# One decoder step: first unit of each feed-forward stage as eight plain products, and the second gated group brought in by quadrants

## The reference

```python
def conv_ffn(h, prev, w_up, conv_w, conv_b, w_down):
    l = h.shape[1]
    u = h @ w_up
    ext = jnp.concatenate([prev, u], axis=1)
    y = conv_b + sum(conv_w[k] * ext[:, k:k + l] for k in range(CONV_WIDTH))
    a, v = jnp.split(y, 2, axis=-1)
    return (jax.nn.silu(a) * v) @ w_down, ext[:, -(CONV_WIDTH - 1):]
```

## Time and profile before

| | |
|---|---|
| median of 3 runs | 3003.3 us (2996.12 to 3003.37) |
| the profiled execution | 3006.05 us |
| its span in the trace | 3004.0 us |
| its mean granted PE clock | 0.96 |
| PE busy | 2792.8 us, 93% |
| DVE busy | 1877.8 us, 63% |
| ACT busy | 1227.7 us, 41% |
| POOL busy | 1192.5 us, 40% |

### The profile page before, as it was taken

One profiled execution on the slowest core, in us unless ns is written; L12 is line 12 of the kernel. 1 busy time (PEld: TensorE's weight loads), 2 busy tenths in 40 slices (PEclk: granted clock), 3 DMA queues, 4 the chain that ended last, 5 costly groups with the idle time before them and its releaser, 6 DMA issues. The chain is left out here.

```text
span 3004.0 us, 54687 instructions
## 1 busy us (share of the span) xinstructions
PE 2792.8 (93%) x20984; PEld 2564.1 (85%) x20984; DVE 1877.8 (63%) x3428; ACT 1227.7 (41%) x2492; POOL 1192.5 (40%) x786
## 2 busy tenths in 40 slices
PE   8998979999989996999999799899978999998898
PEld 7996966666767796999999799897878999998898
DVE  6212148888545526788887766695356777777665
ACT  5002027777723314554545333314234455444332
POOL 4430000000000143445455778560334555547876
PEclk9999989999979998999999999999988999998999
DMA  6216750000357420222222222312101222232222
GB/s 187 55 42 229 238 179 4 2 2 2 126 153 220 131 78 24 71 81 83 69 83 105 100 87 70 133 41 116 43 31 58 83 71 85 83 108 103 82 79 88
DMA packets 163911, 272.16 MB, mean 91 GB/s; under 512 B 19510, under 2 KB 112028, under 8 KB 162480
## 3 DMA queue, kind: packets, MB, share of 16 engines
q1 hardware_dynamic: 137348, 225.19, 22.5%
q10 hardware_dynamic: 26316, 43.66, 4.4%
HBM read 226.22 MB, written 46.69 MB: 91 GB/s over the span
## 5 line engine op out<-in xcount | busy, mean ns | idle before, releaser
L3065 PE MATMUL banks<-token_blocks_high,weight_blocks_high 128*128 128x272 f32 x3696 | 780.5, 293 | 108.2 <-DVE x L3359 35.0
L3065 PE MATMUL banks<-token_blocks_low,weight_blocks_high 128*128 128x272 f32 x3696 | 771.4, 291 | 0.0
L3065 PE MATMUL banks<-token_blocks_high,weight_blocks_low 128*128 128x272 f32 x3696 | 771.3, 291 | 0.0
L3065 PEld LDWEIGHTS banks<-token_blocks_high,weight_blocks_high 128*128 128x128 f32 x3696 | 587.5, 192 | 120.0 <-issue 83.8
L3065 PEld LDWEIGHTS banks<-token_blocks_low,weight_blocks_high 128*128 128x128 f32 x3696 | 589.8, 192 | 0.0
L3065 PEld LDWEIGHTS banks<-token_blocks_high,weight_blocks_low 128*128 128x128 f32 x3696 | 587.4, 192 | 0.0
L2975 POOL TENSOR_TENSOR weight_blocks_low<-weights_again_whole,weight_blocks_high 128x512 fp32r<-128x512 f32 (+2 forms) x151 | 228.0, 1513 | 195.3 <-ACT weight_blocks_high L3089 195.0
L2975 POOL TENSOR_TENSOR weight_blocks_low<-weights_whole,weight_blocks_high 128x512 fp32r<-128x512 f32 (+2 forms) x151 | 217.6, 1447 | 204.2 <-ACT weight_blocks_high L3089 202.7
L3321 DVE SCALAR_TENSOR_TENSOR conv_space<-conv_space,conv_w 128x1024 f32<-128x1024 f32 x176 | 230.3, 1308 | 77.5 <-ACT conv_space L3146 66.0
L2975 POOL TENSOR_TENSOR weight_blocks_low<-ight_quarters_more,weight_blocks_high 128x512 fp32r<-128x512 f32 (+2 forms) x150 | 211.9, 1415 | 155.5 <-ACT weight_blocks_high L3089 154.6
L3359 DVE TENSOR_TENSOR x<-x,banks 128x544 f32<-128x544 f32 x224 | 160.4, 718 | 172.4 <-PE banks L3065 169.1
(11 more groups left out here) (512 smaller groups left out, 5310.8 us busy)
## 6 DMA issues: line engine op xcount, KB each, us to landing
gated_scratch<-conv_space ACTq DMA_DIRECT2D x44, 544.0 KB, 3.9
past_rows<-in_kv_pages SPq DMA_DIRECT2D x160, 128.0 KB, 2.4
ight_quarters_more<-in_w_up SPq DMA_DIRECT2D x56, 256.0 KB, 3.0
weights_whole<-in_w_up SPq DMA_DIRECT2D x56, 256.0 KB, 2.9
weights_again_whole<-in_w_up SPq DMA_DIRECT2D x56, 256.0 KB, 2.9
staged<-gated_scratch SPq DMA_DIRECT2D x8, 1632.0 KB, 8.6
z<-in_kv_pages SPq DMA_DIRECT2D x96, 128.0 KB, 2.4
x<-in_cmp_pages ACTq DMA_DIRECT2D x64, 128.0 KB, 5.8
```

Source lines behind the costliest of these rows:

```text
L3065: last = pe.matmul(out[:, piece, :], a[:, at], b[:, kk, piece * HP:(piece + 1) * HP], start=first and kk == 0 and z == 0, stop=kk == n - 1 ...
```

## The change

- **Unit 0** is made of 8 plain products: `first_unit` multiplies x1, x3, x2, x4 in this order with two quarters of weights each, 192 matmuls where 168 were. Its four weight blocks are plain quarters; `project` rounds and splits all four ahead of layer 0's stage and two ahead of layer 1's (`blocks_ready`), the other two come at the stage's start. Results go to `ext` by four copies of ACT (`copy_first`); there is no `place` for unit 0.
- The norm's multiplications and the tokens' low parts for unit 0 are made by rows and half quadrants (`norm_rows`, `lower_rows`). The four **token sums** are made behind them, for unit 1 on.
- **Unit 1** is no longer interleaved with unit 0; only units 20 and 21 are (`LEAD`, `LAST`). ACT does unit 0's two taps between the rounding of the third and fourth token sums, its silu and store during unit 1.
- **Weight sums** of unit 1 and of unit 21 are made by POOL (`SUMMED_BY_POOL`), those of units 2 to 20 by DVE as before.
- **Staging** of groups 1 to 3: four transfers, one per quadrant, each with its semaphore; DVE's and ACT's waits are for their own quadrant. The tables for the way from group 0 to group 1 have other numbers.
- Places in memory and bank numbers move (`UP_PLACE`, `DOWN_SLOTS`, `Y_AT`, `bank_set`).

```diff
+Y_AT = -(-2 * EXT // 8) * 8
 CHUNK = -(-TH // P)
 
-UP_PLACE = (0, 1, 3, 2, 4, 6, 5)
-DOWN_SLOTS = (4, 2, 3, 5, 8, 6, 7, 0, 1)
+UP_PLACE = (0, 1, 6, 3, 4, 2, 5)
+DOWN_SLOTS = (8, 4, 5, 3, 2, 6, 7, 0, 1)
...
         self.raw = place("tokens_unsplit", [ROWS_UP, TH], offset=self.tl_at)
+        self.blocks_ready = 4 if layer == 0 else 2
...
+    def split_first(self, pool, w, loaded, blocks):
+        for n in blocks:
...
+            pool.tensor_tensor(low, self.first_block(w, n), high.bitcast(F32), ALU.subtract).then_inc(self.w_split, 1)
...
+        LEAD, FIRST_PRODUCTS, FIRST_BLOCKS = LAST - 1, 8, 4
+        PRODUCTS = FIRST_PRODUCTS + BLOCKS * (UNITS - 1)
+        SUMMED_BY_POOL = {1: 0, LAST: 1}
...
-        UP_RAW = {0: x1, 1: x3, 2: t2_raw, 3: raw[:, KH * UP_PLACE[3]:KH * UP_PLACE[3] + KH, :], 4: x2, 5: x4, 6: x3}
+        FIRST = ((x1, up_block(0)), (x3, up_block(1)), (x2, (up_block(4)[0], y_low)), (x4, up_block(5)))
+        UP_RAW = {2: t2_raw, 3: x1, 4: x2, 6: x3}
...
@@ -2930,9 +2938,10 @@
                 else:
                     sp.wait_ge(d_split, BLOCKS * p)
                 n, at = PAIRS[p], starts[p]
-                for half in range(2):
-                    src = g_dram[at + half * n:at + (half + 1) * n].rearrange("k p t -> p k t")
-                    sp.dma_start(staged[:, half * n:(half + 1) * n, :], src).then_inc(staged_loaded, 16)
+                for cols in range(2):
+                    for kk in range(2):
+                        src = g_dram[at + kk * n:at + (kk + 1) * n, :, cols * TH:cols * TH + TH].rearrange("k p t -> p k t")
+                        sp.dma_start(gated_quadrants(p)[2 * kk + cols], src).then_inc(staged_loaded[2 * kk + cols], 16)
...
+            pool.wait_ge(normed, KH)
+            f.split_first(pool, w, 0, range(f.blocks_ready, FIRST_BLOCKS))
+            first_sums(1)
+            for q in range(1, UNITS):
+                if q == 1:
+                    lower(1, 0)
+                    lower(1, 1)
+                    second_sums(1)
+                    for j in range(2, BLOCKS):
+                        lower(1, j)
...
+            def first_unit():
+                for t, (_, (high, low)) in enumerate(FIRST):
+                    pe.wait_ge(w_split, 2 if t == 0 else FIRST_BLOCKS)
+                    if t == 2:
+                        pe.wait_ge(normed, KH + 6)
+                    for kk in range(KH):
+                        pe.wait_ge(split, KH * t + kk + 1 if t == 0 else KH + 2 * (t - 1) + kk // 2 + 1)
+                        for out in range(2):
+                            wh, wl = f.ring(t % 2 * 2 + out, KH * P)
+                            at = slice(kk * P, (kk + 1) * P)
+                            for z, (a, b) in enumerate(((wh, high), (wh, low), (wl, high))):
+                                for piece in range(2):
+                                    last = pe.matmul(k.ps[:, 2 * (t // 2 * 2 + out) + piece, 0:HP], a[:, at], b[:, kk, piece * HP:(piece + 1) * HP],
+                                                     start=t % 2 == 0 and kk == 0 and z == 0, stop=t % 2 == 1 and kk == KH - 1 and z == 2,
+                                                     skip_group_check=True)
+                            if kk == KH - 1:
+                                last.then_inc(multiplied, 1)
+
...
+            def round_sum(j):
+                act.wait_ge(made, (3, 2, 4, 6).index(j) + 1)
+                if j == 4:
+                    wait_product(act, 0, 5)
+                act.activation(up_block(j)[0], UP_RAW[j], ACT.Copy).then_inc(up_rounded, 1)
+
+            def copy_first(what):
+                n = ("C11", "C21", "C12", "C22").index(what)
+                wait_product(act, 0, 2 + n % 2 + 4 * (n // 2))
+                act.activation(in_two(ext[:, n % 2, 2 + n // 2 * TH:2 + n // 2 * TH + TH]), k.ps[:, 2 * n:2 * n + 2, 0:HP], ACT.Copy).then_inc(copied, 1)
...
+            copy_first("C11")
+            copy_first("C21")
+            round_weights(0)
+            round_weights(1)
+            round_sum(3)
+            round_sum(2)
+            act.wait_ge(constants_loaded, 16 * 3)
             round_weights(2)
             round_weights(3)
-            f.scale(act, KC - 1).then_inc(gained, 1)
-            round_tokens(0)
-            round_tokens(1)
-            round_tokens(2)
-            copy(0, "V1")
-            round_weights(4)
-            round_weights(5)
-            round_tokens(3)
-            round_weights(6)
-            round_weights(7)
-            round_tokens(4)
-            act.wait_ge(constants_loaded, 16 * 3)
-
-            for n in range(4, BLOCKS * FC):
+            round_sum(4)
+            copy_first("C12")
+            copy_first("C22")
+            tap(0, 0)
+            tap(0, 1)
+            round_sum(6)
+
+            for n in range(BLOCKS * (FC - 1)):
                 q, j = at_place(n)
-                if j == 0 and q not in FOLLOWS:
+                if j == 0 and q != LAST:
                     copy(q, "V1")
...
                     if p + 1 < len(PAIRS):
-                        for j, at in enumerate((19, 20, 25, 25, 26, 27, 27) if p == 0 else (7, 9, 23, 23, 24, 26, 27)):
+                        for j, at in enumerate((14, 15, 24, 25, 26, 27, 27) if p == 0 else (7, 9, 23, 23, 24, 26, 27)):
                             if i == at:
...
             dve.wait_ge(gained, 1)
-            norm(x3, 0)
-            dve.wait_ge(rstd_copied, 1)
-            norm(x4, 1)
-            lower(1)
+            halves = (slice(0, 2), slice(2, 4))
+            for t in range(1, 4):
+                if t == 2:
+                    dve.wait_ge(spreaded, 2)
+                norm_rows(t, halves[0])
+                norm_rows(t, halves[1])
+                lower_rows(t, halves[0], KH + 2 * t - 1)
+                lower_rows(t, halves[1], KH + 2 * t)
+            difference(x1, x2, x1, made)
+            wait_product(dve, 0, 5)
+            difference(t2_raw, x4, x1, made)
+            difference(x2, x4, x2, made)
             dve.drain()
-            dve.tensor_tensor(x2, x2, over_half(v[:, 1, :]), ALU.mult).then_inc(normed, 1)
-            difference(UP_RAW[3], x2, x1, made)
-            difference(t2_raw, x4, UP_RAW[3], made)
-            difference(x2, x4, x2, made)
             lower(2)
             lower(3)
+            lower(4)
+            difference(x3, x3, t2_raw, made)
+            lower(6)
             dve.memset(ext[:, 0, 0:2], 0.0)
...
-            first_sums(1)
-            second_sums(1)
-            for q in range(FC):
-                if q and q not in FOLLOWS:
+            convolve_first()
+            for q in range(1, FC):
+                if 1 < q < LAST:
...
                     if p + 1 < len(PAIRS):
-                        early = (20, 21, 21, 22, 22) if p == 0 else (9, 11, 12, 14, 16)
-                        late = (24, 25, 26, 27) if p == 0 else (21, 23, 24, 25)
+                        early = (15, 16, 18, 20, 21) if p == 0 else (9, 11, 12, 14, 16)
+                        late = (23, 25, 26, 27) if p == 0 else (21, 23, 24, 25)
```

293 lines of the change are left out of this document (133 added, 160 removed).

## The result

| | before | changed |
|---|---|---|
| median | 3002.88 us (8 runs, 2996.12 to 3009.42) | 2988.59 us (8 runs, 2984.32 to 2990.22) |
| ratio | | 0.9949, 95% interval 0.9939 to 0.9958 |
| profiled execution, its span | 3006.05, 3004.0 us | 2988.75, 2986.9 us |

The change is worth 14.3 us by the medians. The forecast was 2999.8, with a range of 2985 to 3011 that takes in half of rival B; the forecast's own range, 2991 to 3008, was missed by 2.4 us.

The account below looks back on a forecast made before the run. PE bounds the kernel wherever it has operands, so its waits, matmul count and low clock decide. 3006.05 + 6.5 (heads) - 10 (way to group 1 with quadrants) = 3002.5, median 2.75 below: 2999.8 us; range 2985 to 3011, own 2991 to 3008.

Parts of the forecast that it names:

- rival B: Heads and way to group 1: POOL and DVE turns do not add up, about 2978, half of it 2989 to 2990; chance 0.18.
- the way to group 1: Group 0 to group 1: waits of 2.9 and 3.4 us replace one of 8.84, 8.9 against 13.25, -4.4 per layer.
- The head of layer 0: Units 0 and 1, layer 0: three old waits go, one long one comes; 72.9 against 71.3 us, +1.6.
- V1 wait: Before unit 1's third product: PE waits 16.0 us for ACT's copy, a 28.0 us chain less 11.9 of cover.
- six turns: DVE's passes in the head: each of six POOL instructions costs DVE a full 1.27 us, 7.6 in all.
- small waits: Layer 0's head: PE waits 2.2 us before x3, 0.9 before x2, 2.9 before unit 1's seventh product.
- The head of layer 1: Units 0 and 1, layer 1: layer 0's +1.6 plus 3.5 us because only two weight blocks are ready, +5.1.
- POOL's two splits: Layer 1's head: POOL makes two weight blocks, x3 1.2 and x2 1.3 us later, 1.0 more of low clock.
- the quadrants: Staging by four transfers: ACT starts when the first quadrant lands; -0.6 us per layer, between 0 and -1.9.
- Signs: Traces: V1 wait 13 to 19 us, DVE rows 2.4 to 2.9, POOL 2.5 or more, two middle waits about 3.
- C: Way to group 1 saves nothing, a wait before product 23 replaces the one before 24; 3009.8 us, up to 3014; chance 0.15.
- D: Staging: all four quadrant transfers land together, the first semaphore no sooner; +1 to +2, 3001.5 us; chance 0.10.

Follow-up runs that it names:

- changed_again: The changed kernel run once more, unaltered, against the kernel before: 2986.15 us against 3000.98, ratio 0.9956 (0.9940 to 0.9972).
- short_sums: Changed kernel with two of POOL's weight sums of unit 1 made over 32 of 512 columns: 2980.91 us against 3002.88 before, ratio 0.9927.
- middle_only: Kernel before with the new group 0 to group 1 tables and four-quadrant staging, no new head: 2987.90 us against 3000.98, ratio 0.9956.
- tables_only: Kernel before with only the new tables for the way from group 0 to group 1: 2998.78 us against 3004.96, ratio 0.9989.
- head_only: Changed kernel with the old tables and old two-part staging, so only the new first unit: 3000.35 us against 3004.96 before, ratio 0.9987.
- both_early: copies_early plus DVE's first convolution and place(1, C11) ahead of its last low part, that sum's rounding between ACT's taps: 2977.98 us against 3002.88 before, ratio 0.9916.
- copies_early: Changed kernel with ACT's copies V1, V2 of unit 1 and three weight roundings ahead of unit 0's taps: 2977.69 us against 3004.96 before, ratio 0.9920.

## Why the prediction was right or wrong

The time lay in the stated range, 11 us under the value, and only because that range took in half of rival B. I had called the change none, within 0.3% of before, with a chance of 0.60; it was faster by 0.5%, to which I gave 0.27. Of the 11 us some 6.5 are the heads, 2 the norm's factors and 3 the way to group 1. That three errors the same way stayed inside the range is luck.

- **The head of layer 0**, forecast +1.6: measured +0.4 in the first trace (71.4 against 71.0) and -1.1 in `changed_again`. The mechanism was right in each step. The V1 wait was 14.7 for a forecast of 16.0: six turns at 1.27 were the mis-sized term, they cost 0.97 (`short_sums`). What ACT does behind them took 5.9, as forecast, and the four products that cover it 11.9. The small waits were 1.7, 2.2 and 2.2, forecast 2.2, 0.9 and 2.9. Low clock in the head was some 6.0 (PE busy 50.66 for 44.7 us of matmuls), forecast 6.2, and 4.4 in `changed_again`.
- **The head of layer 1**, forecast +5.1: measured -0.4. I had added 3.5 for POOL's two splits: 1.2 before x3, 1.3 before x2, and 1.0 of low clock. POOL does take DVE's turn, as the low parts of x3 show, layer 0 and layer 1 of the changed kernel:

```profile
1151.22 2.49 DVE L3281 TENSOR_TENSOR token_blocks_low<-tokens_unsplit,token_blocks_high 128x1088 fp32r<-128x1088 f32 x2
...
2223.49 4.47 DVE L3281 TENSOR_TENSOR token_blocks_low<-tokens_unsplit,token_blocks_high 128x1088 fp32r<-128x1088 f32 x2
```

  And PE is late by as much: counted from the first product it starts x3 after 8.8 us (7.9 in layer 0) and x2 after 18.4 (16.4), 2.0 late for a forecast of 2.5. The step that failed is that low clock comes on top of this. PE from the start of x3 and from the start of x2, layer 0, then layer 1 (columns as in the earlier trace rows):

```profile
1152.66:1158.91 6.25, 6.25 (x48) 6.04 (x48) 6.25 (x6) 2.23 (x2) 0.00 (x0) 1.00 0.01 3
1161.09:1168.98 7.89, 7.89 (x51) 7.89 (x52) 4.80 (x4) 2.78 (x5) 0.11 (x1) 0.78 0.00 0
2225.82:2233.59 7.77, 7.77 (x48) 7.56 (x48) 7.77 (x6) 2.23 (x2) 0.99 (x1) 0.78 0.00 0
2235.33:2241.67 6.34, 6.34 (x51) 6.34 (x52) 4.80 (x4) 2.78 (x5) 0.11 (x1) 1.00 0.01 3
```

  Layer 0 has its 1.5 us of low clock behind the wait for x2, layer 1 behind the longer wait for x3 (2.58 against 1.69), where DVE is late in any case, and none behind x2's (1.74). So most of the 2.0 is back when DVE's chain starts, and V1's wait ends 0.4 later than in layer 0 (51.25 against 50.81 from the first product). The other traces with the new head have layer 1's low clock at the same place. I also set the head of before to 71.3 for both layers; it was 72.1 in layer 1.
- **Ahead of the head**: 1.0 us a layer was not in the sum. The row was in the trace of before (1.25 for 32 columns, when the pass of 512 ahead of it takes 0.69), and I did not ask what lengthened it.
- **The way to group 1, and the quadrants**: together forecast -10, measured 0.9956 with `middle_only`, so some -13 (-8 to -18), and 5.4 a layer in the length of the windows with about 1.7 more to the end of part 1. The sum was near, its division wrong. I gave the tables 4.4 a layer and the quadrants 0.6, from ACT's wait of 1.90 for group 2. Alone the tables gave some 3.3 in both layers and the quadrants nothing. The step that failed is that the moved passes were costed without the transfer that they now reach first: group 1's was in time for the old table, and as two halves it is 2.2 us late for the new one (`tables_only`). Of the waits, the 3.4 before the next part's third product was 3.30; before product 23 it was 1.81 for POOL's low block, where I had 2.9 for DVE's addition.
- **Signs.** The V1 wait lay in the 13 to 19 named, in both layers (14.7). POOL's six took 2.4 (the first two) to 3.4 us for the 2.5 or more named; DVE's were 3.3 to 3.5 where I had named 2.4 to 2.9, since I had not put the wait for POOL inside its duration. The waits in the middle, 1.81 and 3.30, stayed under 6. The matmul groups grew by 16 if unit 0's own (L3070, x128) is counted with the x3584.
- **Rivals.** B's time (2989 to 2990 for half of it) was hit by chance, its reason not: POOL and DVE do take turns. C (the way to group 1 gives nothing) is excluded by `middle_only`; D (quadrants do nothing) holds with the old tables and fails with the new.

That the heads gain nothing by one product more and three waits less is shown by `head_only`; what is left of its 3.9 us (0 to 7.5) beside the 2.0 of the norm's factors is within the interval. That those 2.0 reach the time of the whole kernel is argued from the traces; no run takes them away alone.

## What to carry to other kernels

Two edits that look independent can each be worth little and much together: when passes are moved earlier, look first at which transfer they now meet, and try the two edits apart and joined before giving the gain to either. When one long wait takes the place of several, follow the copy that releases it through its engine's list, but expect the wait to turn up again behind the next bound: moving the copies put 8.4 of 14.7 us before a later product, and the 4.5 and 4.2 us that those five lines gained a head came with POOL's blocks, which no longer ran beside DVE's convolution. And compare a stretch of two traces only from its own first instruction, and two heads only where low clock falls at the same place: traces of the same code lay up to 7.7 us apart ahead of the head, and 1.5 inside it.

## What the hardware showed

- A DVE scaling of 32 columns, one tensor in SBUF times a scalar per partition, took 1.25 us beside POOL and 0.24 without it, so not only passes over two tensors are held up. PE's wait behind two of them fell by 1.0 us, 3.34 to 2.33. A convolution step over 64 columns (L3368) took 1.30 beside POOL and 0.28 without.
- One POOL instruction of 512 columns cost a DVE pass of 2176 columns 0.97 us on average, less than POOL's own 1.26 alone.
- The same wait of PE, 2.17 to 2.21 us before x2 in layer 0, was followed by a granted clock of 0.73 over the next 6.3 us in four traces and by 1.00 in four. Layer 1's wait of 2.53 to 2.72 before x3 was followed by 0.78 over x3's products in all eight, and its wait of 1.72 to 1.75 before x2 by 1.00 in all eight.
- Less idle time need not be less time: `both_early` has 3.07 us less of it than `copies_early` in layer 0, in waits of 3.10, 3.60 and 2.97 for 3.09, 8.37 and 1.27, and PE's busy time is 2.28 more for the same matmuls. Layer 1 of the same pair gives 2.7 less idle and 2.66 more busy. It is one pair of traces, though both have low clock behind x2's wait in layer 0, so the size is open.
